# Hybrid decoder step: gate broadcasts and sample attention placed in other stages, second doubled expert one place later

## The chip, the core and the metric

The kernel runs on one core of a Trainium2 chip. The metric is the time on the device of one whole step, in microseconds (us), as the median of several runs. TensorE (PE) does the matrix products into eight PSUM banks, VectorE (DVE) and ScalarE (ACT) read the banks out and do the element work, GpSimd (POOL) does small copies and issues DMAs, SyncE (SP) issues the weight loads. Everything is float32.

## What is computed

One layer for 256 prompt rows and 8 x 4 sample rows, width 2048, cut to the parts that matter here:

```python
h = layernorm(x) * (1 + sc1) + sh1
q, k, v, u = split(h @ w_in)
attn = window_attention(q, k, v, cache)                  # sample rows: 8 requests x 4 positions
z = gelu(s5(u))
ssm = z * sigmoid(z @ ssm_glu_w + ssm_glu_b)
mixed = concat(rms(attn) * attn_norm_g, rms(ssm) * ssm_norm_g)
o = mixed @ w_out
x = layernorm(alpha * x + g1 * o) * ln1_g + ln1_b        # g1: the gate, one row per request
h2 = layernorm(x) * (1 + sc2) + sh2
# mixture: best group of 4, then the best 2 of its 8 experts, 288 rows x 2 = 576 pairs over 32 experts
f = sum_e comb[:, e] * ((silu(h2 @ w_gate[e]) * (h2 @ w_up[e])) @ w_down[e])
x = layernorm(alpha * x + g2 * f) * ln2_g + ln2_b
```

## The kernel before

The program is written out by hand for each engine, with semaphores between them; the order of the code is the order of the queue. The weights pass in 1 MB chunks through a ring: six slots up to the experts, twelve for them. SP loads a chunk when the PE has counted the old one off on the semaphore `used`.

The stages around the change, on the PE:

- **glu stage.** `glu_part(m)`, m = 0 to 7, is one eighth of `z @ ssm_glu_w` (eight matmuls of 128x288, L2346). ACT's `glu_gate(m)` takes the sigmoid (L1271), DVE's `ssm_gated(m)` the product (L1763, L1766) and POOL its square (L1087). After the fourth part stand the turns of q (L2289) and the scores of the sample rows (L2362, L2363), after the eighth the turns of the sample probabilities (L2372).
- **first output projection.** `project(q, half)` is half of the inner width for 512 columns of `mixed @ w_out`: sixteen 128x512 matmul records for the two prompt blocks (L2395) and eight for the samples, four 32-column pieces beside each other (L2398). q = 0 to 3 take the ssm half of `mixed`, and q = 4 to 7 the attention half. q = 0 is run first, both halves.
- **between it and the heads.** Eight matmuls with a column of ones sum the squares of the ssm half (L2435). Then a loop over x = 0 to 7 does three things. It broadcasts the gate g1 over the partitions, for x = 0 to 3 from 32 rows of `MOD` into bank 7 (L2450) and for x = 4 the sample gates (`by_quarters`, L2443), each copied out by ACT into `GX` or `GXs` (L1310) before the next may overwrite the bank. It multiplies the sample probabilities with the cached and the new values of request x (L2457, L2458) into banks 0 to 3. In two of its turns it also adds up the four sample pieces (`sum_parts(0)`, L2406) and turns the row of squares (L2465). After the loop comes one `ada_step` (L348, the weights of the later modulation), then `scores(0)` and `scores(1)` (L2384), which wait until DVE has read the sample attention out (`so_ready`, L1811), and then `project(1, 0)`.
- **heads.** Eight units of prompt attention, each with a half projection, ada steps and turns, up to the second half of the output projection.

DVE reads the sample attention first (L1811), then adds the projection of the prompt blocks (`blocks_out(0)`, L1853 and L1863), then that of the samples (`samples_out(0)`), then the heads.

**Experts.** Each pass of the expert loop is one block of up to 64 rows of one expert: L792 gate and up products, L754 and L761 the gathering of the next block's rows by a selection matrix, L770 their turns, L800 and L809 the down product. Where an expert has more than 64 rows, its second block uses the same weights, and the ring's slots are counted free in the second one only. The order of the experts is by a key: an expert's number, and for the w-th doubled expert WIDE_FROM + WIDE_STEP * w. Experts without rows are left out.

Of the kernel before, what the change touches and what calls it, by code (L numbers as in the profile page):

```python
# [20 lines left out]
ALU = mybir.AluOpType  # L21
ACT = mybir.ActivationFunctionType
AX = mybir.AxisListType

P = 128
# [23 lines left out]
WIDE_FROM, WIDE_STEP = 4.5, 6.0  # L49
# [161 lines left out]
def build(nc, a, o, scratch):  # L211
# [11 lines left out]
    with ExitStack() as ctx:  # L223
# [204 lines left out]
        GX, GXs = later[:, 6144:8192], later[:, 8192:8704]  # L428
# [17 lines left out]
        g_q, b_q = L[:, 8704:9216], L[:, 9216:9728]  # L446
        dot, sq_junk, w_s = L[:, 9728:10752].rearrange("p (i n) -> p i n", i=2), L[:, 10752:11264], L[:, 11264:11776]
# [523 lines left out]
        with nc.Block() as block:  # L971
# [31 lines left out]
            def _(pool):  # L1003
# [96 lines left out]
                for r, x in enumerate(("ln1_g", "ln1_b")):  # L1100
                    pool.dma_start(R4[r:P:NS, :], a[x].rearrange("o (q n) -> (o q) n", q=4)).then_inc(S("r4_in"), 16)
                for x, t in (("ln1_g", g_q), ("ln1_b", b_q)):
# [22 lines left out]
            def _(act):  # L1125
# [148 lines left out]
                for m in range(4):  # L1274
                    glu_gate(m)
# [4 lines left out]
                glu_gate(4)  # L1280
                glu_gate(5)
                act.wait_ge(S("snegmax_ready"), 1)
# [4 lines left out]
                glu_gate(6)  # L1287
                glu_gate(7)
# [14 lines left out]

                act.wait_ge(S("kv_out"), 16 * 20)
                parts_out(0)
                act.wait_ge(S("ssm_ready"), 16)
                act.wait_ge(S("state_out"), 64)
                for i in range(5):
                    act.wait_ge(S("gx_ps"), i + 1)
                    nc.scalar.copy(GX[:, 512 * i:512 * i + 512] if i < 4 else GXs, bank[:, 7, :])\  # L1310
                      .then_inc(S("gx_ready"), 1)
                act.wait_ge(S("rs_ms"), 2)
                nc.scalar.activation(srms[:, :], srms[:, :], ACT.Sqrt).then_inc(S("rs_sqrt"), 1)
# [50 lines left out]
                for i in range(2):  # L1364
                    if i:
                        act.wait_ge(S("kc_ready"), since("kc_ready") + 1)
                    nc.scalar.activation(L[:, 9728:11776], GEf[:, D * i:D * i + D], ACT.Square, accum_out=kc[:, 2 + i:3 + i])\
# [73 lines left out]
            def _(dve):  # L1441
# [365 lines left out]
                dve.wait_ge(S("so_ps"), 1)  # L1807
                for g in range(NKV):
                    r = slice(32 * g, 32 * g + 32)
                    src = bank[r, 0:4, :].rearrange("p j (b n) -> p (j b) n", b=2)[:, :, HD * g:HD * g + HD]  # L1810
                    V.tensor_tensor(OS[r, :, :], src, spread(sden[r, :], HD), ALU.mult).then_inc(S("so_ready"), 1)  # L1811
# [897 lines left out]
```

## Time and profile before

| | us |
|---|---|
| median of 3 runs | 1620.47 |
| lowest and highest | 1614.94, 1621.84 |
| the profiled execution | 1620.20 |
| its span, first to last instruction | 1618.4 |
| PE busy in it | 1499.4 (93%) |
| DVE, ACT, POOL busy | 509.3, 287.2, 142.3 |

Starts are counted in us from the first instruction. The loops and the stages follow each other in time: up to about 341 the front of the layer, 341 to 380 the glu stage, 380 to 396 the first output projection, 396 to 430 the loop of small products, 430 to 676 heads, projection and router, 676 to 1566 the 31 expert blocks, then the last norm.
### The profile page before, as it was taken

The numbers are of one execution on the slowest core, as the hardware profiler recorded it, in microseconds if no ns is written. First come the engines' busy times: TensorE is split into PE (matmuls) and PEld (weight loads), VectorE is DVE, ScalarE is ACT, GpSimd is POOL, SyncE is SP. The second block draws the span as 40 slices with busy tenths as digits, with TensorE's granted clock in tenths as the row PEclk, the third lists the DMA queues.
The fourth block names the chain that finished last, engine by engine and source line by source line (L and its number), as shares of the span: only waits on it lengthen the run. The fifth ranks groups of instructions, "written<-read, shape, count | busy, mean of one in ns | idle before, by whom it ended". The sixth has DMA issues, their size and how long they took to land.

```text
span 1618.4 us, 22163 instructions
## 1 busy us (share of the span) xinstructions
PE 1499.4 (93%) x8151; PEld 641.5 (40%) x8152; DVE 509.3 (31%) x1446; ACT 287.2 (18%) x669; POOL 142.3 (9%) x213
## 2 busy tenths in 40 slices
PE   3899999999999899899999999999999999999974
PEld 2457544455444345333333333333333333333321
DVE  6648354322233356721121212112121211211216
ACT  2221240132222322121121201001010100100111
POOL 6001000320300230000000000000000000000011
PEclk9999999999699899899999999999999999999997
DMA  9995888973287789899999989999799999999955
GB/s 300 387 386 181 305 323 311 316 197 104 61 302 290 290 300 396 359 411 422 421 422 421 378 333 422 422 421 422 297 406 421 421 421 422 422 421 422 421 234 222
DMA packets 119286, 559.66 MB, mean 346 GB/s; under 512 B 15657, under 2 KB 20553, under 8 KB 64921
## 3 DMA queue, kind: packets, MB, share of 16 engines
q1 hardware_dynamic: 100800, 510.20, 79.1%
q0 software_dynamic: 17952, 46.05, 8.4%
q10 hardware_dynamic: 482, 2.70, 0.6%
q8 instruction: 34, 0.56, 0.1%
q14 instruction: 18, 0.15, 0.0%
HBM read 565.78 MB, written 42.37 MB: 376 GB/s over the span
## 4 chain that ended last, share of the span: by engine, by line
PE 79%; DMA 13%; DVE 4%; ACT 2%; issue 1%; POOL 0%; POOLq 0%; SPq 0%; DVEq 0%; ACTq 0%
PE bank L792 24%; PE bank L809 11%; DMA ring<-in_exp_w_up 8%; PE bank L2395 6%; PE bank L754 6%; PE bank L2303 5%; PE bank L2153 4%; PE bank L348 3%; DMA ring<-in_w_in 2%; PE bank L2346 2%; DMA ring<-in_ada_w 2%; PE bank L761 2%; DVE BC L610 1%; PE bank L800 1%; PE bank L2235 1%
## 5 line engine op out<-in xcount | busy, mean ns | idle before, releaser
L792 PE MATMUL bank<-ring,BC 128*64 128x512 f32 x1984 | 473.8, 596 | 5.5 <-DMA ring<-in_exp_w_up 3.2
L792 PEld LDWEIGHTS bank<-ring,BC 128*64 128x64 f32 x1984 | 151.1, 137 | 301.2 <-issue 279.1
L809 PE MATMUL bank<-ring,BC 128*64 128x512 f32 x992 | 219.7, 595 | 16.6 <-ACT BC L715 16.6
L589 DVE COPY MOD<-bank 128x512 f32<-128x512 f32 x32 | 22.1, 692 | 430.3 <-PE bank L761 430.3
L754 PE MATMUL bank<-H,MOD 128*64 128x512 f32 x512 | 132.9, 592 | 0.3 <-DVE H L2013 0.3
L809 PEld LDWEIGHTS bank<-ring,BC 128*64 128x64 f32 x992 | 70.8, 137 | 142.5 <-issue 142.5
L545 POOL DMA_INDIRECT y_dram<-BC,y_row x31 | 29.9, 965 | 947.7 <-DVE y_row L619 862.7
L2395 PE MATMUL bank<-ring,MT 128*128 128x512 f32 x224 | 101.6, 607 | 1.0 <-issue 0.8
L703 ACT COPY MOD<-bank 128x512 f32<-128x512 f32 x32 | 18.7, 585 | 461.9 <-PE bank L761 461.9
L2303 PE MATMUL bank<-ring,MT 128*128 128x512 f32 x192 | 85.4, 598 | 1.0 <-ACT X L1228 1.0
L616 DVE COPY BC<-bank 128x512 f32<-128x512 f32 x31 | 21.4, 692 | 166.1 <-PE bank L809 166.1
L2153 PE MATMUL bank<-MT,ring 128*128 128x288 f32 x256 | 66.0, 421 | 6.3 <-DMA ring<-in_w_in 4.0
L754 PEld LDWEIGHTS bank<-H,MOD 128*64 128x64 f32 x512 | 41.2, 137 | 73.0 <-issue 71.8
L348 PE MATMUL bank<-ring,cT 128*32 128x512 f32 x512 | 65.0, 625 | 0.0
L2395 PEld LDWEIGHTS bank<-ring,MT 128*128 128x128 f32 x224 | 42.2, 193 | 55.4 <-issue 54.8
L2153 PEld LDWEIGHTS bank<-MT,ring 128*128 128x128 f32 x256 | 50.1, 197 | 21.8 <-issue 5.3
L610 DVE TENSOR_TENSOR BC<-BC,bank 64x512 f32<-64x512 f32 x31 | 21.4, 691 | 111.6 <-ACT BC L713 111.6
L719 ACT COPY BC<-bank 128x512 f32<-128x512 f32 x31 | 18.1, 585 | 212.2 <-PE bank L809 212.2
L2303 PEld LDWEIGHTS bank<-ring,MT 128*128 128x128 f32 x192 | 35.6, 190 | 48.1 <-issue 46.9
L2131 PE MATMUL bank<-ring,cT 128*32 128x512 f32 x256 | 36.1, 659 | 19.4 <-DMA ring<-in_ada_w 19.0
L770 PEld LDWEIGHTS bank<-con,MOD 128*128 128x128 f32 x256 | 33.3, 210 | 26.9 <-issue 25.1
L770 PE MATMUL bank<-con,MOD 128*128 128x128 f32 x256 | 39.4, 297 | 0.9 <-DVE MOD L589 0.9
(561 smaller groups left out, 1465.5 us busy)
## 6 DMA issues: line engine op xcount, KB each, us to landing
ring<-in_exp_w_gate SPq DMA_DIRECT2D x128, 1024.0 KB
ring<-in_exp_w_up SPq DMA_DIRECT2D x128, 1024.0 KB
ring<-in_exp_w_down SPq DMA_DIRECT2D x128, 1024.0 KB
ring<-in_ada_w SPq DMA_DIRECT2D x96, 1024.0 KB
ring<-in_w_in SPq DMA_DIRECT2D x20, 1024.0 KB
y_dram<-con POOLq DMA_DIRECT2D x20, 1024.0 KB, 34.2
ring<-in_w_out SPq DMA_DIRECT2D x16, 1024.0 KB
ring<-in_ssm_glu_w SPq DMA_DIRECT2D x4, 1024.0 KB
```

The source lines that it names most:

```text
L348: mm = pe.matmul(bank[32 * g:32 * g + 32, b, :], cT[:, k, :], w[:, 512 * g:512 * g + 512], start=(k == k0), stop=(k == k1))
L610: V.tensor_tensor(AC[hi, :], SG[hi, :], bank[hi, 2, :], ALU.mult).then_inc(S("act_ready"), 1)
L754: pe.matmul(bank[64 * h:64 * h + 64, i, :], sel[:, b, :], H[:, b, 512 * q:512 * q + 512], start=(b == 0), stop=False)
L761: mm = pe.matmul(bank[64 * (q % 2):64 * (q % 2) + 64, q // 2, :], sel[r, 2, :], H[r, 2, 0:512], start=False, stop=True)
L770: mm = pe.transpose(bank[:, i, P * k:P * k + P], XG[:, i, k:512:4], ident)
L792: mm = pe.matmul(bank[64 * i:64 * i + 64, 2, :], xT[:, q // 2, k % 4, 64 * (q % 2):64 * (q % 2) + 64], ring[:, at, 512 * (k % 4):512 * (k ...
L809: mm = pe.matmul(bank[64 * (c % 2):64 * (c % 2) + 64, 4 + c // 2, :], aT[:, j, :], ring[:, at, 512 * c:512 * c + 512], start=(j == 0), sto ...
L2131: mm = pe.matmul(bank[32 * g:32 * g + 32, 4 + v, :], cT[:, 4 * i + g, :], w[:, g, :], start=(i == 0), stop=(i == 3))
L2153: mm = pe.matmul(bank[:, 4 * half + m, 0:T], w[:, k, P * m:P * m + P], MT[:, 4 * j + k, :], start=(j == 0 and k == 0), stop=(j == 3 and k ...
L2303: pe.matmul(bank[:, b, :], MT[:, 4 * i + k, P * b:P * b + P], w[:, k, :], start=(i == 0 and k == 0), stop=(i == 3 and k == 3))
L2346: mm = pe.matmul(bank[:, 4 + m % 2, 0:T], w[:, k, P * (m % 2):P * (m % 2) + P], Z[:, k, :], start=(k == 0), stop=(k == 7))
L2395: pe.matmul(bank[:, x, :], MT[:, k0 + k, P * b:P * b + P], w[:, k, :], start=(half == 0 and k == 0), stop=(half == 1 and k == 3))
```

## The change

It keeps every product, and moves them:

- The four broadcasts of the gate stand behind `glu_part(2)`, `(3)`, `(4)` and `(5)`, that of the samples behind `glu_part(6)`. ACT copies them between its sigmoids. `GX` lies in other columns of the ring (four separate pieces), since the glu stage still uses its old place; `b_q`, `dot` and the junk tile of the squares move likewise, and POOL waits once for `state_out` before it loads over the old state columns.
- The sample attention products stand inside `project(0, 0)` (requests 0 and 1) and `project(0, 1)` (2 to 5), one behind each inner step, and 6 and 7 behind it. The sums of the squares stand between the two halves.
- `scores(0)` and `scores(1)` stand inside `project(1, 0)`, behind its second inner step. The wait for `x_smp` moves from ahead of `project` to ahead of its sample matmuls.
- DVE does `blocks_out(0)` ahead of the reading of the sample attention, and ACT the root of the ssm scale ahead of `parts_out(0)`.
- WIDE_FROM, WIDE_STEP go from 4.5, 6.0 to 2.5, 8.0.

PE, from the first output projection to the ada step behind the loop (its last product being row L348), before. `bank` is PSUM, `MT` the mixed rows turned, `con` the constants, `BC`, `H` and `X` hold probabilities and values:

```order
L2395 MATMUL bank<-ring,MT 128x512 x8
L2398 MATMUL bank<-ring,MT 32x512 x4
L2395 MATMUL bank<-ring,MT 128x512 x8
L2398 MATMUL bank<-ring,MT 32x512 x4
L2435 MATMUL bank<-H,con 1x288 x8
L2450 MATMUL bank<-MOD,con 128x512
L2457 MATMUL bank<-BC,H 128x256
L2458 MATMUL bank<-X 128x256
L2406 MATMUL bank<-BC 32x512
L2450 MATMUL bank<-MOD,con 128x512
L2457 MATMUL bank<-BC,H 128x256
L2458 MATMUL bank<-X 128x256
```

The same place with the change, from the sample matmuls of the first half on:

```order
L2438 MATMUL bank<-ring,MT 32x512 x4
L2498 MATMUL bank<-H,con 1x288 x8
L2431 MATMUL bank<-ring,MT 128x512 x2
L2469 MATMUL bank<-BC,H 128x256
L2470 MATMUL bank<-X 128x256
L2431 MATMUL bank<-ring,MT 128x512 x2
L2469 MATMUL bank<-BC,H 128x256
L2470 MATMUL bank<-X 128x256
L2488 MATMUL bank<-con,H 128x1 x3
L2431 MATMUL bank<-ring,MT 128x512 x2
L2469 MATMUL bank<-BC,H 128x256
L2470 MATMUL bank<-X 128x256
```

The 32-row broadcasts are gone from here, and each pair of small products has two 128x512 matmuls of the projection on either side.

PE, the end of the glu stage with the change, where before the four L2346 parts stood in one piece (a row of 32):

```order
L2358 MATMUL bank<-ring 128x288 x8
L2376 MATMUL bank<-MOD,con 128x512
L2358 MATMUL bank<-ring 128x288 x8
L2376 MATMUL bank<-MOD,con 128x512
L2358 MATMUL bank<-ring 128x288 x8
L2366 MATMUL bank<-MOD,con 32x512 x4
L2358 MATMUL bank<-ring 128x288 x8
```

A broadcast now stands behind each part but the last.

DVE, which frees the banks that the next projection writes, before:

```order
L1811 TENSOR_TENSOR BC<-bank,sden 32x512 [waits so_ps,dve_self]
L1811 TENSOR_TENSOR BC<-bank,sden 32x512 x3
L1853 SCALAR_TENSOR_TENSOR BC<-bank,srms,ring 128x512 [waits used,gx_ready,xa_in]
L1863 SCALAR_TENSOR_TENSOR ring<-ring,BC 128x512 [waits out_free]
L1853 SCALAR_TENSOR_TENSOR BC<-bank,srms,ring 128x512 [waits dve_self]
```

and with the change:

```order
L1864 SCALAR_TENSOR_TENSOR BC<-bank,srms,ring 128x512 [waits gx_ready,used,xa_in,dve_self]
L1874 SCALAR_TENSOR_TENSOR ring<-ring,BC 128x512 [waits out_free]
L1864 SCALAR_TENSOR_TENSOR BC<-bank,srms,ring 128x512 [waits dve_self]
L1874 SCALAR_TENSOR_TENSOR ring<-ring,BC 128x512 [waits out_free]
L1822 TENSOR_TENSOR BC<-bank,sden 32x512 [waits so_ps,dve_self]
L1822 TENSOR_TENSOR BC<-bank,sden 32x512 x3
```

The two groups have changed places.

The diff, cut to its core:

```diff
-WIDE_FROM, WIDE_STEP = 4.5, 6.0
+WIDE_FROM, WIDE_STEP = 2.5, 8.0
...
-        GX, GXs = later[:, 6144:8192], later[:, 8192:8704]
+        GX = [later[:, at:at + 512] for at in (4608, 5120, 5632, 9216)]
+        GXs = later[:, 9728:10240]
...
+                def gx_out(i):
+
+                    act.wait_ge(S("gx_ps"), i + 1)
+                    nc.scalar.copy(GX[i] if i < 4 else GXs, bank[:, 7, :]).then_inc(S("gx_ready"), 1)
+
+                glu_gate(0)
+                glu_gate(1)
+                glu_gate(2)
+                gx_out(0)
+                glu_gate(3)
+                gx_out(1)
...
                 glu_gate(4)
+                gx_out(2)
                 glu_gate(5)
+                gx_out(3)
...
                 glu_gate(6)
+                gx_out(4)
                 glu_gate(7)
...
+                act.wait_ge(S("rs_ms"), 2)
+                nc.scalar.activation(srms[:, :], srms[:, :], ACT.Sqrt).then_inc(S("rs_sqrt"), 1)
                 act.wait_ge(S("kv_out"), 16 * 20)
                 parts_out(0)
...
                 blocks_out(0)
+                samples_attended()
                 samples_out(0)
...
                 for m in range(4):
                     glu_part(m)
+                    if m >= 2:
+                        gx_in(m - 2)
...
                 for m in range(4, 8):
                     glu_part(m)
+                    if m < 7:
+                        gx_in(m - 2)
...
-                def project(q, half):
+                def project(q, half, between=None):
...
+                        if between:
+                            between(k)
+                    if half == 0 and 0 < q < 4:
+                        pe.wait_ge(S("x_smp"), q)
...
+                project(0, 0, first_samples)
+                for m in range(8):
+                    pe.wait_ge(S("sq_ready"), m + 1)
+                    mm = pe.matmul(bank[0:1, 3, 0:T], ones[:, 0:1], gate[:, m, :], start=(m == 0), stop=(m == 7))
+                mm.then_inc(S("rs_ps"), 1)
+                pe.wait_ge(S("ssm_ready"), 16)
+                project(0, 1, middle_samples)
+                pe.wait_ge(S("rs_ms"), 2)
+                samples_attend(6)
+                samples_attend(7)
+                pe.wait_ge(S("sum4_ready"), 1)
+                sum_parts(0)
                 pe.wait_ge(S("gx_ready"), 5)
                 for v, k in ADA_FIRST:
                     ada_step(pe, v, k, 7)
...
-                        project(q, i % 2)
+                        project(q, i % 2, None if i else first_scores)
```

## Rows read from the trace of the kernel before

**Rows 1.** The page: clock granted to the PE in 40 slices of 40.5 us.

```profile
PEclk9999999999699899899999999999999999999997
```

**Rows 2.** Timeline of PE, 396 to 454: start us, us, engine, line, product, records [idle before <-releaser].

```profile
396.37 4.04 PE L2435 MATMUL bank<-H,con 128*1 128x288 f32 x16
400.34 1.12 PE L2450 MATMUL bank<-MOD,con 32*128 32x512 f32 x2
401.39 0.70 PE L2457 MATMUL bank<-BC,H 128*128 128x256 f32 x2
...
402.65 1.05 PE L2406 MATMUL bank<-BC 128*32 128x512 f32 x2
...
426.68 3.09 PE L2384 MATMUL bank<-H,GE 64*128 64x128 f32 x16 [1.14 <-DVE BC L1811]
430.52 8.95 PE L2395 MATMUL bank<-ring,MT 128*128 128x512 f32 x16 [0.75 <-issue]
...
440.29 1.04 PE L348 MATMUL bank<-ring,cT 128*32 128x512 f32 x8
...
444.73 1.16 PE L2384 MATMUL bank<-H,GE 64*128 64x128 f32 x8
445.82 7.13 PE L2395 MATMUL bank<-ring,MT 128*128 128x512 f32 x16
...
453.88 0.44 PE L2415 MATMUL bank<-con,X 128*128 128x128 f32 x2
```

**Rows 3.** Stretches: length, busy us (records) of PE, PEld, DVE, ACT, POOL, PEclk, DMA share, GB/s.

```profile
400.00:405.00 5.00, 5.00 (x14) 1.61 (x12) 0.61 (x2) 0.80 (x2) 0.00 (x0) 1.00 0.21 81
405.00:410.00 5.00, 5.00 (x18) 2.12 (x16) 0.16 (x1) 0.95 (x2) 0.00 (x0) 0.69 0.00 0
415.00:420.00 5.00, 5.00 (x10) 2.00 (x8) 0.18 (x1) 2.90 (x4) 0.00 (x0) 0.50 0.00 0
...
430.00:435.00 5.00, 4.48 (x6) 1.98 (x7) 4.65 (x13) 1.74 (x9) 5.00 (x9) 0.58 0.17 20
```

**Rows 4.** Timeline of PE: turns of the next rows (L770), one row per expert block.

```profile
696.78 1.23 PE L770 MATMUL bank<-con,MOD 128*128 128x128 f32 x8
...
893.83 1.23 PE L770 MATMUL bank<-con,MOD 128*128 128x128 f32 x8
...
923.59 1.23 PE L770 MATMUL bank<-con,MOD 128*128 128x128 f32 x8
...
1374.09 1.23 PE L770 MATMUL bank<-con,MOD 128*128 128x128 f32 x8
...
1403.85 1.23 PE L770 MATMUL bank<-con,MOD 128*128 128x128 f32 x8
...
1556.07 1.23 PE L770 MATMUL bank<-con,MOD 128*128 128x128 f32 x8
```

**Rows 5.** Stretches of one block's length in the experts, columns as in rows 3.

```profile
921.98:950.13 28.15, 27.28 (x133) 9.92 (x131) 5.01 (x16) 2.62 (x5) 0.96 (x1) 1.00 0.63 244
...
1147.18:1175.33 28.15, 27.27 (x135) 10.19 (x133) 5.01 (x16) 2.62 (x5) 0.96 (x1) 1.00 0.60 239
```

**Rows 6.** Timeline of PE: a broadcast by quarters at the full clock.

```profile
570.80 1.06 PE L2443 MATMUL bank<-MOD,con 32*32 32x512 f32 x8
```

**Rows 7.** Timeline of PE in the middle of the glu stage.

```profile
357.20 1.04 PE L2289 MATMUL bank<-con,X 128*128 128x128 f32 x8
...
360.65 0.45 PE L2362 MATMUL bank<-ring,X 64*32 64x128 f32 x8 [1.75 <-POOL X L1082]
...
363.10 15.79 PE L2346 MATMUL bank<-ring 128*128 128x288 f32 x64
```

**Rows 8.** Timeline of ACT: one copy of a gate broadcast.

```profile
401.58 0.58 ACT L1310 COPY ring<-bank 128x512 f32<-128x512 f32 x1 [4.32 <-PE bank L2450]
```

**Rows 9.** Timeline of DVE behind the loop of small products.

```profile
423.78 2.84 DVE L1811 TENSOR_TENSOR BC<-bank,sden 32x512 f32<-32x512 f32 x4 [6.93 <-PE bank L2458]
426.66 0.75 DVE L1853 SCALAR_TENSOR_TENSOR BC<-bank,srms,ring 128x512 f32<-128x512 f32 x1
427.44 0.69 DVE L1863 SCALAR_TENSOR_TENSOR ring<-ring,BC 128x512 f32<-128x512 f32 x1
```

More of the change, by code:

```diff
@@ L1806, in _, with samples_attended @@
                 go(V.reciprocal(srms[:, :], srms[:, :]))
[L1807 to L1811, printed above, removed]
+                def samples_attended():
+                    dve.wait_ge(S("so_ps"), 1)
+                    for g in range(NKV):
+                        r = slice(32 * g, 32 * g + 32)
+                        src = bank[r, 0:4, :].rearrange("p j (b n) -> p (j b) n", b=2)[:, :, HD * g:HD * g + HD]
+                        V.tensor_tensor(OS[r, :, :], src, spread(sden[r, :], HD), ALU.mult).then_inc(S("so_ready"), 1)
                 def head(i):
@@ L2348, in glu_part, with by_quarters, gx_in @@
                     mm.then_inc(used if m % 2 else S("glu_ps"), 1)
+                def by_quarters(b, v, at):
+                    for g in range(4):
+                        r = slice(32 * g, 32 * g + 32)
+                        mm = pe.matmul(bank[r, b, :], con[r, C_SEL + at:C_SEL + at + NS], MOD[r, v, :], start=True, stop=True)
+                    return mm
+                def gx_in(x):
+                    if x:
+                        pe.wait_ge(S("gx_ready"), x)
+                    else:
+                        pe.wait_ge(S("y_free"), 8)
+                    if x < 4:
+                        mm = pe.matmul(bank[:, 7, :], con[32 * x:32 * x + 32, C_SEL:C_SEL + P],
+                                       MOD[32 * x:32 * x + 32, 0, :], start=True, stop=True)
+                    else:
+                        mm = by_quarters(7, 0, P)
+                    mm.then_inc(S("gx_ps"), 1)
                 pe.wait_ge(S("z_ready"), 2)
@@ L2424, in samples_in, with samples_attend @@
                     mm.then_inc(S("mt_ps"), 1)
[L2426 to L2455 removed]
+                def samples_attend(x):
                     out = bank[:, x // 2, 256 * (x % 2):256 * (x % 2) + 256]
@@ L2458, in _, with first_samples, middle_samples @@
                     mm = pe.matmul(out, PTn[:, x, :], qkv[0:NS, 2, DA + DKV:DA + 2 * DKV], start=False, stop=True)
-                    if x == 0:
-                        pe.wait_ge(S("sum4_ready"), 1)
-                        sum_parts(0)
-                    if x == 1:
+                    if x == 7:
+                        mm.then_inc(S("so_ps"), 1)
+                def first_samples(k):
+                    if k == 1:
+                        pe.wait_ge(S("spt_ready"), 4)
+                        samples_attend(0)
+                    elif k == 2:
+                        samples_attend(1)
+                def middle_samples(k):
+                    samples_attend(2 + k)
+                    if k == 1:
                         pe.wait_ge(S("rs_ms"), 1)
@@ L2467, in _ @@
                         rs.then_inc(S("rs_ps"), 1)
-                mm.then_inc(S("so_ps"), 1)
+                pe.wait_ge(S("glu_sig"), 8)
+                pe.wait_ge(S("mod_ready"), 2)
+                pe.wait_ge(S("ssm_ready"), 8)
+                project(0, 0, first_samples)
[10 more added lines that the diff above has]
+                sum_parts(0)
                 pe.wait_ge(S("gx_ready"), 5)
@@ L2471, in _, with first_scores @@
                     ada_step(pe, v, k, 7)
+                def first_scores(k):
+                    if k == 1:
+                        scores(0)
+                        scores(1)
                 unit_end = {4: KD - 1, 5: ADA_LAST[0][1] - 1}
-                scores(0)
                 for i, (n, g) in enumerate(UNITS):
-                    if i < 7:
+                    if 0 < i < 7:
                         scores(i + 1)
```

49 lines of the change are left out of this document (6 added, 43 removed).

## The prediction

> **What bounds the kernel now.** I read the page's clock row first: the PE is busy 93% of the span, so time is lost where it works slowly. One slice early in the program stands at 6 tenths, the eleventh, 405 to 445 us [rows 1]. The stretches of 5 us say where: the PE is busy without a gap from 400 to 420, yet its granted clock is 1.00 up to 405, 0.69 in the next 5 us, 0.50 at 415 (1.2 GHz, the lower of its two levels) and still 0.58 at 430 to 435 [rows 3]. The timeline shows what it did before: from 396.37 on it ran the sums with a column of ones, then 32-row broadcasts and 256-column products, and nothing dense until `project(1, 0)` at 430.52 [rows 2]. That projection took 8.95 us there and 7.13 at 445.82. So from 396.37 to 440.29, 43.92 us, the bound is the PE at a low clock, and at the end of it two small waits, 1.14 us for DVE's reading of the sample attention and 0.75 us. DMA moves nothing there (share 0.00), since the ring is full.
>
> The experts are the second place. The turns of one block follow those of the next after 28.15 us while the PE is the bound: from 923.59 to 1374.09 there are 16 steps, 450.50 us. From 1403.85 to 1556.07 there are five, 30.44 us each: there the weights bound, 2.29 us more per block. Two single steps, 893.83 to 923.59 and 1374.09 to 1403.85, are 29.76 us, 1.61 over the fast pace [rows 4]. The DMA share falls to 0.63 and 0.60 in two stretches 225 us apart [rows 5]: the doubled experts, whose first block frees no slot. DMA idles 10.4 us in the first and 11.3 us in the second. Nothing between the two stages waits on a date: each load goes by `used`, so what the front gains, the end gains.
>
> **The change part by part.** I sum the profiled execution, 1620.20 us against a median of 1620.47.
>
> *The stretch 396.37 to 440.29.* The same work at the full clock, from rows at 1.00: sums with ones 3.97 (to the next start, 400.34); eight pairs of sample products, each 402.65 - 401.39 = 1.26, together 10.1; the three tiny turns of the square row about 0.3; `sum_parts(0)` 1.05; ada step 1.04; two `scores`, each 445.82 - 444.73 = 1.09, together 2.2; `project(1, 0)` as its neighbour, 453.88 - 445.82 = 8.06 [rows 2]. Sum 26.7. Against 43.9 this takes off 17.2.
>
> *The broadcasts in the glu stage.* Four of 1.05 (401.39 - 400.34) [rows 2] and one by quarters of 1.06 [rows 6]: 5.3 us are added, since the PE has no idle time there that could hide them, except 1.75 us ahead of the sample scores. That wait is no cover: it ends with POOL's copies, which follow ACT's copies of the turned q, and ACT now does one gate copy of 0.58 [rows 8] ahead of those. I add 0.3 (bounds 0 and 0.6). The other ACT copies fall between sigmoids that are 3.9 us apart (15.79 for four parts, [rows 7]), and bank 7 is free long before the next broadcast.
>
> *New waits.* The sample products wait for ACT's copies of the turned probabilities, a full inner step of the projection earlier than they are asked for. The turn of the squares waits for DVE's copies, with two inner steps and two pairs, some 6 us, as cover. `scores(0)` waits for `so_ready`: with P the end of `project(0, 1)`, DVE does four operations of 0.75 and 0.69 (3.0 us), then the four reads, 2.84 us [rows 9], done at P + 5.9. The PE has two pairs (2.5), the sum and the ada step (2.1) and half a projection (3.6) ahead of it, so it asks at P + 8.2: 2.3 us of cover. `out_free` is there at P + 2.3, asked at P + 4.6. Queued behind DVE's wait for `so_ps` are `samples_out(0)` and the first head; `project(1, 0)` asks for `x_smp` only at its samples, some 6 us later. POOL's sample DMAs start later against the projection by some 5 us, and the sample heads are wanted five units on. I cost all of it at nothing. If the cover failed everywhere, 3 us would go back, my upper bound.
>
> *The order of the experts.* The key of the w-th doubled expert goes from 10.5 and 16.5 to 10.5 and 18.5. By the reference's routing of these inputs experts 1 and 6 are doubled (97 and 101 pairs) and 18 has no rows, so the first stays ninth in line and the second passes expert 17 only: one place. After a full ring eight blocks run at 28.15, the ninth waits 1.61, each further one 2.29: so it is from the start (696.78 to 893.83, seven steps of 28.15, then 29.76) and behind the second doubled expert [rows 4]. Before: 1.61 once, then none ahead of the second, then 1.61 and five of 2.29, 14.7 us. After: 1.61 three times (the second doubled expert's first block is now a ninth one) and four of 2.29, 14.0 us. It gains 0.7; the difference of the two idle times, 0.9, says the same. Bounds: 0 and 2.3, one late block.
>
> Sum: -17.2 + 5.3 + 0.3 - 0.7 = -12.3 us. 1620.5 - 12.3 = **1608.2 us**, some 1608.
>
> *A rule against it.* What decides is why the clock fell, and the row shows it falling with no idle time on the PE [rows 3]. The Trainium skill, page "TensorE: Matmul & The Clock Gate", section "Why this matters for your kernels", says that drops amid a kernel are avoided by leaving no idle gaps between bursts of matmuls; by that rule the order of busy work is nothing to the clock. The trace does not agree: no gap, and 0.50. If something else than the kind of work drives it, the change moves work from slow to slow, and that is the second rival.
>
> **The rivals.**
>
> *The clock falls behind the first projection after all.* Two pairs, the sum and the ada step are still light, 4.6 us, and half of `project(1, 0)` comes before more. Price: 4.6 us more for them and 1.8 for the projection (8.95 against 7.13). Gain 5.9: 1614.6. For it: 4 us of ones and then ten of light work brought the fall. Against: the light stretch from 440.29 to 445.82 (ada steps, turns, scores) is 5.5 us and the projection behind it ran in 7.13 [rows 2].
>
> *The fall does not come from the small products.* Then the slow stretch stays with this part of the program, and only the two waits (1.9), the experts (0.7), less 0.3, are gained: 1618.2. For it: the broadcasts and products are counted as full busy time. Against: the lone stretch at 0.50 is the one without dense work.
>
> *The glu stage loses its clock.* Its light part, 357.20 to 363.10, 5.9 us at full clock [rows 7], has a 32-row broadcast ahead of it now. A fall near its end costs its last 2 us and the first 2.6 of the next part, some 4 us: 1612.
>
> *Slower.* The pairs between the steps of `project(0, 1)` bring the clock down inside it. Then 8.06 of projection, six pairs (7.6), the square turns, the sum and the ada step (2.4) run at half speed, 18 us more, and 1.8 in `project(1, 0)`. Net +7.5: 1628. It decides from the point where more than 12.3 us of this work run at 1.2 GHz, so the fall must come before the third inner step. Against: each 1.26 us pair has 1.8 us of dense work on either side, and one dense projection (8.95 us, from 430.52) was enough to bring the clock back before.
>
> **How the numbers follow.** Forecast 0.71, the fall behind the projection 0.10, no clock gain 0.06, a fall in the glu stage 0.07, slower 0.05, more than I sum (other low slices, such as the fourteenth, shift too) 0.01. The forecast's own range is 1605 to 1611: the bounds above and the spread of medians. To hold 8 in 10 the range takes in the glu case and reaches to the first rival: 1604 to 1615. A measurement of this kernel tells some 0.5%, 8.1 us, from no change: faster is under 1612.4, the forecast and most of the glu case, 0.76; within 0.5% the two clock rivals and the rest, 0.19; slower 0.05.
>
> **What would show it.** PEclk's eleventh slice at 9; stretches at 1.00 from 385 to 430; the first projection from some 386, `project(1, 0)` over 11.6 us earlier than 440.29; broadcasts at 1.05 us in the glu stage; no wait at the first `scores`; the wait of 1.75 at about 2.0; the second dip of the DMA share one block later against the first, and four slow blocks at the end for five. Wrong would make it a clock under 1.00 in the glu stage or the first projection, or a wait of the PE for `so_ready`.

## The result and the profile after

The changed kernel takes 1608.71 us (median of 8 executions, 1607.57 to 1612.44); the kernel before 1621.55 (8, 1614.94 to 1623.4). The ratio is 0.9929, 95% interval 0.9919 to 0.9939. The forecast was 1608 with a range of 1604 to 1615.

The profiled execution took 1608.62, its span 1606.8 against 1618.4. The page's clock row, changed kernel:

```profile
PEclk9999999999999898899999999999999999999987
```

The eleventh slice, the 6 of [rows 1], is a 9. The stretches of 5 us (columns as in [rows 3]):

```profile
400.00:405.00 5.00, 5.00 (x15) 2.18 (x14) 0.61 (x2) 0.00 (x0) 0.00 (x0) 1.00 0.27 115
405.00:410.00 5.00, 5.00 (x19) 2.83 (x19) 0.34 (x2) 0.20 (x1) 0.00 (x0) 1.00 0.00 0
415.00:420.00 5.00, 5.00 (x20) 1.91 (x20) 4.77 (x8) 1.40 (x2) 0.00 (x0) 1.00 0.70 229
...
430.00:435.00 5.00, 5.00 (x36) 2.88 (x36) 1.22 (x3) 0.59 (x1) 0.16 (x1) 1.00 0.92 367
```

PE is busy throughout in both kernels up to 420; what changed is the granted clock, 1.00 where [rows 3] has 0.69 and 0.50. The timeline of PE of the changed kernel, beside [rows 2] and [rows 7]:

```profile
341.57 11.88 PE L2358 MATMUL bank<-ring 128*128 128x288 f32 x48 [0.40 <-issue]
353.38 1.12 PE L2376 MATMUL bank<-MOD,con 32*128 32x512 f32 x2
354.43 4.15 PE L2358 MATMUL bank<-ring 128*128 128x288 f32 x16
...
359.56 1.09 PE L2301 MATMUL bank<-con,X 128*128 128x128 f32 x8
...
363.07 0.45 PE L2396 MATMUL bank<-ring,X 64*32 64x128 f32 x8 [1.75 <-POOL X L1083]
...
365.51 4.15 PE L2358 MATMUL bank<-ring 128*128 128x288 f32 x16
369.59 1.12 PE L2376 MATMUL bank<-MOD,con 32*128 32x512 f32 x2
...
386.57 3.60 PE L2431 MATMUL bank<-ring,MT 128*128 128x512 f32 x8
...
402.72 0.59 PE L2469 MATMUL bank<-BC,H 128*128 128x256 f32 x2
403.24 0.69 PE L2470 MATMUL bank<-X 32*128 32x256 f32 x2
403.87 1.98 PE L2431 MATMUL bank<-ring,MT 128*128 128x512 f32 x4
...
418.68 3.70 PE L2431 MATMUL bank<-ring,MT 128*128 128x512 f32 x8
422.31 1.71 PE L2420 MATMUL bank<-H,GE 64*128 64x128 f32 x16
423.95 3.70 PE L2431 MATMUL bank<-ring,MT 128*128 128x512 f32 x8
...
428.46 1.04 PE L348 MATMUL bank<-ring,cT 128*32 128x512 f32 x8
```

The ada step behind `project(1, 0)` starts at 428.46, 11.83 us ahead of the 440.29 of [rows 2]. The scores at 422.31 have no wait in front of them.

**Most of the gain is clock.** Each execution comes with its span and its mean granted clock. Span x (1 - mean clock), called "missing" below, adds up the clock that was not granted; span x mean clock is the rest. (The clock is given to 0.001, which is 1.6 us, so only medians of several executions are worth reading.) Over all executions taken of both kernels in this study:

| | executions | span, us | mean clock | missing, us | span x mean clock, us |
|---|---|---|---|---|---|
| before | 66 | 1618.8 (1610.3 to 1624.3) | 0.971 (0.966 to 0.978) | 47.0 | 1571.5 |
| changed | 12 | 1606.9 (1605.7 to 1610.6) | 0.9785 (0.975 to 0.981) | 34.6 | 1572.3 |

The two kernels differ in the missing clock and hardly in the rest. The measure is rough, since it covers the whole program and also counts a low clock while PE waits, which costs nothing. In the two traces it falls by only 6.7 us (mean clock 0.972 and 0.976) for 11.6 us of span: from 396 to 441 the clock goes from 0.70 to 1.00, but behind the last full turns of the expert loop it is 0.78 before (from 1556) and 0.73 with the change (from 1544). The time that the low clock cost is read from the stretch itself: 43.92 us from 396.37 to 440.29, less 1.9 of waits and less 32.0 of work at the full clock (the 26.7 of the prediction and 5.3 of broadcasts), leaves 10.0 us. So of the 11.6 some 10 are clock, and 1.9 are the waits that went; the smaller terms nearly cancel. The spread of the kernel before, 14 us, goes with the clock as well: its quickest execution has the highest mean clock.

### The profile page after: what moved, and what is told of

It reads as the page before. It is cut to its first block, busy times and chain, and to the rows that moved or that the text cites. A ratio compares the mean times of both kernels' runs of the same rounds, so it can differ in the third digit from the quotient of the medians.

```text
span 1606.8 us, 22161 instructions
## 1 busy us (share of the span) xinstructions
PE 1493.3 (93%) x8151; PEld 645.8 (40%) x8152; DVE 509.9 (32%) x1446; ACT 288.0 (18%) x669; POOL 142.6 (9%) x213
## 4 chain that ended last, share of the span: by engine, by line
PE 79%; DMA 13%; DVE 3%; ACT 2%; issue 1%; POOL 0%; SPq 0%; POOLq 0%; DVEq 0%; ACTq 0%
PE bank L793 24%; PE bank L810 11%; DMA ring<-in_exp_w_up 8%; PE bank L2431 6%; PE bank L755 6%; PE bank L2315 5%; PE bank L2165 4%; PE bank L348 3%; DMA ring<-in_ada_w 3%; PE bank L2358 2%; PE bank L762 2%; DMA ring<-in_w_in 2%; DVE BC L611 1%; PE bank L801 1%; PE bank L2143 1%
## 5 line engine op out<-in xcount | busy, mean ns | idle before, releaser
L348 PE MATMUL bank<-ring,cT 128*32 128x512 f32 x512 | 65.2, 620 | 0.0
L2431 PEld LDWEIGHTS bank<-ring,MT 128*128 128x128 f32 x224 | 40.9, 190 | 51.8 <-issue 51.0
L2315 PEld LDWEIGHTS bank<-ring,MT 128*128 128x128 f32 x192 | 35.6, 190 | 48.1 <-issue 46.9
```

The costliest lines, as they stand in the source:

```text
L348: mm = pe.matmul(bank[32 * g:32 * g + 32, b, :], cT[:, k, :], w[:, 512 * g:512 * g + 512], start=(k == k0), stop=(k == k1))
L2315: pe.matmul(bank[:, b, :], MT[:, 4 * i + k, P * b:P * b + P], w[:, k, :], start=(i == 0 and k == 0), stop=(i == 3 and k == 3))
L2431: pe.matmul(bank[:, x, :], MT[:, k0 + k, P * b:P * b + P], w[:, k, :], start=(half == 0 and k == 0), stop=(half == 1 and k == 3))
```

## The experiments

The theory: the light row behind the first output projection (sums with ones, broadcasts, sample pairs, partial sums, ada step) brings the clock down, and the change cuts it up. Rivals: one piece of that row is the cause (the 32-row broadcasts, A; the one-column sums ahead of the rest, C), or the kind of work does not matter. Two lengths in the traces are compared below: the glu stage, up to the start of `project(0, 0)` (38.86 us before, 45.00 with the change), and the stretch from there to the ada step behind `project(1, 0)` (59.82 and 41.89).

**The order of the experts.** `e1_front` is the changed kernel with the old key, `e2_wide` the kernel before with the new one, `e5_after_again` the changed kernel once more, on another chip.

```diff
-WIDE_FROM, WIDE_STEP = 2.5, 8.0
+WIDE_FROM, WIDE_STEP = 4.5, 6.0
```

> The changed kernel with WIDE_FROM, WIDE_STEP back at 4.5, 6.0: the front's moves alone. My theory: all but the experts' part of the gain, so some 1609 us, and in the trace the loop of expert blocks takes as long as before, 859.3 us from the first to the last turn (L771 rows), against 858.2 with the change. Rival, the order of the experts brings the gain: 1620.

> The kernel before with WIDE_FROM, WIDE_STEP 2.5, 8.0 alone. My theory: 0.7 us less, which the times can't tell (1621), and the expert blocks in the trace take 858 to 858.7 us from first to last turn instead of 859.3. Rival: 1610 with the front's gain in it.

> The changed kernel again, beside the kernels that are to be compared with it: 1608 to 1610 us, granted clock 1.00 from 385 to 435 us.

Measured: `e1_front` 1609.8 (10 executions, 1608.05 to 1611.1), ratio 0.9955 (0.9936 to 0.9974); `e2_wide` 1621.61, ratio 1.0015 (0.9997 to 1.0033); `e5_after_again` 1608.62 (4, 1608.42 to 1610.47), ratio 0.9926 (0.99 to 0.9952). From the first full turns of the expert loop to the last, the traces have 859.29 us before [rows 4], 858.94 in `e2_wide`, 858.52 in `e1_front`, and 858.16 and 858.78 in two executions of the changed kernel. Two traces with one key differ by 0.8, as much as the keys do, so what the new key is worth is not shown; expected were 859.3 in `e1_front` and 858 to 858.7 in `e2_wide`. The times came as expected in all three runs, and the gain is in the front. `e1_front` and `e5_after_again` have a stretch of 41.89 us at a clock of 1.00, as in the changed kernel's first trace. The trace of `e2_wide` has the front of before in the same order, and its clock falls later:

```profile
410.00:415.00 5.00, 5.00 (x22) 1.96 (x21) 0.17 (x1) 3.27 (x5) 0.00 (x0) 1.00 0.01 3
415.00:420.00 5.00, 4.87 (x15) 1.38 (x14) 1.83 (x3) 0.52 (x1) 0.00 (x0) 0.59 0.00 0
```

Its stretch is 53.73 us for the 59.82 of [rows 2]. One order of work thus loses 10 us to the clock in one execution and some 4 in another, and one trace can't rank two orders that differ by less.

**Only the broadcasts moved.** `e3_gx_only` is the changed kernel with the broadcasts in the glu stage, and the rest of the front as before: the sums with ones and all eight pairs in a row behind the whole projection, the scores ahead of `project(1, 0)`, DVE and ACT in the old order.

```diff
-                project(0, 0, first_samples)
+                project(0, 0)
+                pe.wait_ge(S("ssm_ready"), 16)
+                project(0, 1)
...
+                for x in range(8):
+                    samples_attend(x)
...
+                scores(0)
```

> Gate broadcasts in the glu stage; the rest of the front as before (sums with ones and all eight pairs of sample products behind the whole first projection, scores ahead of project(1, 0), old order on DVE and ACT), experts as changed. Theory A, the clock fell because of the 32-row broadcasts: it stays at 1.00, the stretch costs its 26.7 us plus 1.9 of waits for DVE, 5.6 in the glu stage: 10 us less than before, 1611. Theory B, it fell because nothing dense ran for about ten us, whatever the small products were: it falls again 9 to 10 us behind the end of the projection, some 10 us of work run at 1.2 GHz, and 1.8 more in project(1, 0): the gain is gone, 1619 to 1622.

Measured: 1617.65 (1615.76 to 1620.66), ratio 0.9996 (0.9978 to 1.0014). Its stretches, with no broadcast anywhere near:

```profile
405.00:410.00 5.00, 5.00 (x17) 1.80 (x16) 0.61 (x2) 0.09 (x1) 0.00 (x0) 1.00 0.50 193
410.00:415.00 5.00, 5.00 (x19) 2.63 (x18) 0.34 (x2) 1.49 (x2) 0.00 (x0) 0.80 0.01 3
415.00:420.00 5.00, 5.00 (x10) 2.40 (x10) 0.00 (x0) 0.00 (x0) 0.00 (x0) 0.50 0.00 0
```

PE has no gap and the clock goes to 0.50 all the same, so the 32-row broadcasts are not needed for the fall, and theory A in its strict form is gone. The median lies between theory A's 1611 and theory B's 1619 to 1622, 2.5 us under the 1620.18 of before on the same chip (missing 43.6 us against 46.9). The broadcasts cost their 5 us in the glu stage as they did in the row, and the ratio's interval takes in 1: a gain from them alone is not shown.

**Only the pairs, sums and scores moved.** `e4_samples_only` is the changed kernel with the five broadcasts behind the projection, between and behind pairs 6 and 7.

```diff
+                gx_in(0)
                 samples_attend(6)
+                gx_in(1)
                 samples_attend(7)
+                gx_in(2)
...
                 sum_parts(0)
+                gx_in(3)
+                gx_in(4)
```

> Sample products, sums with ones and scores inside the projections as changed; the gate broadcasts not in the glu stage but behind the first projection, between the last two pairs and the sum. The broadcasts cost the same 5.3 us there, and DVE's blocks_out(0) waits for the last copy, 2.3 us more on the PE. Theory A (32-row broadcasts): the clock falls in them, 3 to 6 us more: 1614 to 1617. Theory B (a long run without dense work): the light run is 10 us and the wait 2.3, just long enough: also 1612 to 1617. If the clock stays at 1.00: 1611.

Measured: 1611.8 (1610.27 to 1614.6), ratio 0.9948 (0.9929 to 0.9966). The light row is 8.7 us of work and 1.9 of waits, two of them for ACT's copies. The clock is 0.82 in 415 to 420 and 0.50 in 420 to 425, and the first half of `project(1, 0)` takes 5.81 us for 3.70. The median lies by the lower ends of all three expectations, so it does not tell the theories apart:

```profile
416.51 1.06 PE L2363 MATMUL bank<-MOD,con 32*32 32x512 f32 x8 [0.68 <-ACT ring L1279]
418.28 1.93 PE L348 MATMUL bank<-ring,cT 128*32 128x512 f32 x8 [0.70 <-ACT ring L1279]
420.74 5.81 PE L2424 MATMUL bank<-ring,MT 128*128 128x512 f32 x8 [0.53 <-DVE BC L1861]
```

So most of the gain (8 of 12 us) comes from the pairs, sums and scores. The broadcasts' move adds about 3: their 5 us are paid in the glu stage in place of the row, and the waits (1.9) and the last fall (2.1) go.

**All eight pairs in a row.** `e6_row` is the changed kernel with the eight pairs behind the projection; the sums stay between its halves and the broadcasts in the glu stage.

```diff
-                    samples_attend(2 + k)
...
-                samples_attend(6)
-                samples_attend(7)
+                for x in range(8):
+                    samples_attend(x)
```

> The changed kernel with all eight pairs of sample products in a row behind project(0, 1), instead of between its steps; the sums with ones stay between the halves, the broadcasts in the glu stage. Light work behind the projection: samples 1.0, eight pairs 10.1, sum and ada step 2.1, 13 us, none of it a 32-row broadcast. By the theory that the clock falls after some ten us without dense work: it falls near the last pairs, the rest of them and the sum and the ada step (about 4 us) and part of project(1, 0) run slow: 5 to 6 us more than the changed kernel, 1614. If what counts is not the run of light work but its place among other things: 1609.

Measured: 1612.78 (7 executions, 1610.68 to 1615.45), ratio 0.9954 (0.9934 to 0.9973). The size came as expected for a fall in the row, but the trace shows another cause: its row of pairs runs from 410.63 to 422.49 with the clock at 1.00, and the fall stands in the glu stage, at the scores of the sample rows:

```profile
365.00:370.00 5.00, 5.00 (x100) 4.48 (x92) 1.84 (x7) 0.00 (x0) 1.04 (x2) 0.55 0.02 3
415.00:420.00 5.00, 5.00 (x17) 2.36 (x16) 0.00 (x0) 0.00 (x0) 0.00 (x0) 1.00 0.05 17
```

The glu stage takes 47.78 us for 45.00, and the stretch 42.47 for 41.89. The traced execution is the median one (1612.78), so the 4 us over the changed kernel do not show that a row of pairs costs clock; whether it does in the other six executions is open. Theory C, tested below, came from the 1.00 in this row.

**The broadcasts twice.** `e7_gx_twice` issues each of the five broadcasts twice in the glu stage.

```diff
+                    for again in range(2):
```

> Each gate broadcast is issued twice in the glu stage, the first one without effect on the output. If the glu stage has no cover for them, as I summed, 5.3 us more than the changed kernel: 1614. If it hides them (rival): 1609. If the 2.1 us of light work more bring the clock down amid the stage: 1618.

Measured: 1613.74 (1611.05 to 1617.42), ratio 0.9957 (0.994 to 0.9973), 5.1 us over the changed kernel, as expected: nothing in the glu stage covers a broadcast. Four broadcasts went from 1.05 to 1.91 us start to start, the one by quarters from 0.99 to 1.85, so doubling them costs 4.3; the trace's glu stage is 5.85 longer, the rest being a dip of the clock at the sample scores, of which below.

**DVE in the old order.** `e8_dve_old` is the changed kernel with the sample attention read ahead of `blocks_out(0)`.

```diff
-                blocks_out(0)
                 samples_attended()
+                blocks_out(0)
                 samples_out(0)
```

> The changed kernel with DVE in the old order, the reading of the sample attention ahead of blocks_out(0). With P the end of project(0, 1), out_free comes at P + 7.7 instead of P + 2.3 and the PE asks at P + 4.4: a wait of 3.3 us, so 1612. If the PE's idle time adds to the light work before it and the clock falls: 1614 to 1616.

Measured: 1614.09 (1610.51 to 1617.9), ratio 0.9953 (0.9936 to 0.997), 5.5 us over the changed kernel and in the range expected for a wait with a fall of the clock. Timeline of PE:

```profile
416.04 1.44 PE L348 MATMUL bank<-ring,cT 128*32 128x512 f32 x5
420.97 5.40 PE L2431 MATMUL bank<-ring,MT 128*128 128x512 f32 x8 [3.50 <-DVE BC L1864]
```

DVE's reading of the pairs (2.84 us) now stands ahead of the reading of the banks that `project(1, 0)` overwrites. PE waits 3.50 us, and the half projection behind takes 5.40 us for 3.70, at a clock of 0.66 in 420 to 425. So a true gap behind light work lowers the clock too. On this the trace agrees with the row of the Trainium skill that the prediction argued with (page "TensorE: Matmul & The Clock Gate", section "Why this matters for your kernels"); a gap is one way down and not the only one. The swap on DVE, costed at nothing in the prediction, carries 5 us of the gain once the scores are out of the way: without it the cover that the prediction counted on is gone.

**Where the sums stand.** `e9_ones_mid` is the kernel before with only the sums (and the wait for `spt_ready`) moved between the projection's halves. `e10_row_late` is `e6_row` with the sums behind the projection, directly ahead of the pairs.

```diff
                 project(0, 0)
+                pe.wait_ge(S("spt_ready"), 4)
+                for m in range(8):
+                    pe.wait_ge(S("sq_ready"), m + 1)
+                    mm = pe.matmul(bank[0:1, 3, 0:T], ones[:, 0:1], gate[:, m, :], start=(m == 0), stop=(m == 7))
+                mm.then_inc(S("rs_ps"), 1)
                 pe.wait_ge(S("ssm_ready"), 16)
                 project(0, 1)
```

> The kernel before with one edit: the sixteen one-column sums of squares (4.0 us of TensorE) stand between the two halves of the first output projection and not behind it; the five broadcasts, the eight attention pairs, the partial sums and the first ADA products stay behind it in a row, some 19 us at the full clock. Theory C (the clock falls behind the projection because the one-column sums stand directly ahead of more light work; pairs behind dense work alone did not bring it down in the run with all eight pairs in a row): the granted clock stays at 1.00 up to the scores and the time falls by most of the 17 us that the low clock costs, to 1604 to 1608. Theory D (any light row longer than some 12 us brings the clock down): it falls in the last third of the row, 1611 to 1615. Theory A (the 32-row broadcasts bring it down): it falls some 6 us into the row, 1614 to 1618.

> The changed kernel with all eight attention pairs in a row behind the first output projection, as in the run before that had them so, and now the sixteen one-column sums directly ahead of them as well: 4 us of sums, 10 us of pairs, 2 us of partial sums and ADA products, no broadcasts. Only the place of the sums differs from the run with the row (1612.8, clock 1.00 throughout the row). Theory C: the clock falls during the pairs, some 10 us into the light row (409 to 413 us), about 6 us of light work at half speed and a piece of project(1,0): 1617 to 1621. Theory that the place of the sums does not matter: 1612 to 1614 and clock 1.00.

Measured: `e9_ones_mid` 1619.63 (10 executions, 1614.97 to 1622.88), ratio 1.0001 (0.9985 to 1.0017); mean clock 0.971, missing 46.9 us. No theory's range holds it (1604 to 1608, 1611 to 1615, 1614 to 1618). Its clock falls as before:

```profile
405.00:410.00 5.00, 5.00 (x20) 2.16 (x18) 0.16 (x1) 1.17 (x2) 0.00 (x0) 0.87 0.13 48
410.00:415.00 5.00, 5.00 (x14) 1.69 (x14) 0.00 (x0) 0.94 (x2) 0.00 (x0) 0.50 0.02 3
```

`e10_row_late`: 1612.9 (4 executions, 1610.14 to 1619.42), ratio 0.9948 (0.9928 to 0.9969). The traced one is the slowest of the four (span 1617.6, mean clock 0.969) and its pairs slow down from 413.8 on (1.22 us for 0.70); its stretch is 49.99 us. The others have 0.976 to 0.978. Its trace alone would speak for theory C. The medians speak against it: moving the sums by themselves brings nothing in the kernel before, and putting them back costs nothing that four executions can show. As the only cause, the place of the sums is out.

**Broadcasts from all rows.** `e11_gx128` is the kernel before with the four gate broadcasts taken from 128 rows in place of 32. They then give the sum of four quarters of the gate, so the hidden state is another, and the router sends the rows elsewhere: two more expert blocks are computed (2112 records of gate and up products for 1984), and its total of 1671.88 can't be compared.

```diff
-                        pe.matmul(bank[:, 7, :], con[32 * x:32 * x + 32, C_SEL:C_SEL + P],
-                                  MOD[32 * x:32 * x + 32, 0, :], start=True, stop=True).then_inc(S("gx_ps"), 1)
+                        pe.matmul(bank[:, 7, :], con[:, C_SEL:C_SEL + P],
+                                  MOD[:, 0, :], start=True, stop=True).then_inc(S("gx_ps"), 1)
```

> The kernel before with the four gate broadcasts taken from all 128 rows in place of 32 (each then gives the sum of the four quarters of the gate, so this part of the output differs); same order, same column count, same number of instructions. Theory A (few rows lit bring the clock down): clock 1.00 at least until the last broadcast, 4 to 17 us less than before, 1604 to 1617. Theory C (the sums ahead and the length of the row): the clock falls as before near 406, no change, 1620 to 1623.

Its light row has the order and the instructions of before, and no gap up to 418:

```profile
405.00:410.00 5.00, 5.00 (x21) 2.89 (x19) 0.16 (x1) 1.25 (x3) 0.00 (x0) 1.00 0.00 0
410.00:415.00 5.00, 5.00 (x22) 1.92 (x20) 0.17 (x1) 3.46 (x5) 0.00 (x0) 1.00 0.02 3
...
420.00:425.00 5.00, 2.87 (x18) 2.19 (x19) 4.79 (x7) 0.00 (x0) 4.80 (x9) 0.70 0.51 182
```

The clock stays up to the first true wait (2.01 us, ahead of the scores) behind the row. All four executions have a mean clock of 0.975 to 0.979 (missing 39.2 us) where the 13 of the kernel before on this chip have 0.966 to 0.976 (48.5). Up to the scores only the number of rows that four matmuls use was changed, so the mean clocks say that this counts. That rests on four executions, and the trace adds little: its stretch is 53.21 us, and `e2_wide` with the 32-row broadcasts has 53.73 and a clock of 1.00 up to 415. So that the kind of light work counts is likely and not shown beyond doubt.

**What the runs say together.** The light row behind the projection, in us of work at the full clock (for before from the trace of `e11_gx128`, 396.92 to 417.95, and the scores, 1.71), the stretch with its clock in the one trace of each kernel, and the missing clock of the whole program over all executions. Where the broadcasts stand in the row, the stretch holds 5.2 us more of work, and the glu stage as much less:

| kernel | light row | stretch, us | clock in it | executions | missing, us |
|---|---|---|---|---|---|
| before | 22.7 | 59.82 | 0.77 | 66 | 47.0 |
| `e2_wide` | 22.7 | 53.73 | 0.87 | 10 | 51.8 |
| `e11_gx128` | 22.7 | 53.21 | 0.94 | 4 | 39.2 |
| `e9_ones_mid` | 18.7 | 56.92 | 0.82 | 10 | 46.9 |
| `e3_gx_only` | 18.5 | 52.21 | 0.80 | 10 | 43.6 |
| `e10_row_late` | 16.6 | 49.99 | 0.83 | 4 | 38.7 |
| `e6_row` | 11.9 | 42.47 | 1.00 | 7 | 40.3 |
| `e4_samples_only` | 8.7 | 51.30 | 0.93 | 10 | 37.0 |
| changed | 4.4 | 41.89 | 1.00 | 12 | 34.6 |

The clock fell with PE busy in all five traces with 16.6 us or more of light work in a row and 32-row or no broadcasts in it. With PE's order of the changed kernel in the stretch and no new gap it was 1.00 in all five traces (both of the changed kernel, `e1_front`, `e7_gx_twice`, `e12_better`), each 41.89 us long. By this the cause is that the light work stands in a row; neither the broadcasts (`e3_gx_only`) nor the place of the sums (`e9_ones_mid`) is it alone. How long a row may be is not shown: the one trace of `e6_row` holds the clock, and `e4_samples_only` loses it around its waits. The last column moves by other stages too, and by some us between medians of ten (`e2_wide` misses 51.8 with the row of before), so neighbours in it can't be told apart.

**The next light stretch filled.** `e12_better` is the changed kernel, and the main products of `project(4, 0)` stand as four steps between the light work of unit 7.

```diff
+                def last_step(k):
...
+                    w = arrived(pe, first[("out", 0, 0)]).rearrange("p (m n) -> p m n", m=4)
+                    for b in range(2):
+                        pe.matmul(bank[:, b, :], MT[:, k, P * b:P * b + P], w[:, k, :], start=(k == 0), stop=False)
...
+                    if i == 7:
+                        last_step(0)
                     if i:
                         heads_in(i - 1)
+                    if i == 7:
+                        last_step(1)
```

> The changed kernel, and the main products of the first half of project(4,0), which stood behind the last attention unit, are spread as four steps of 0.93 us over the light work of units 6 and 7, where TensorE waits for 0.59, 0.76, 1.16 and 0.59 us at 528 to 538 us and the granted clock is 0.71, 0.50 and 0.77 in the slices from 530 to 543. If the first chunk of the second output weight has landed by 529 us: up to 3.1 us of waits filled and about 3 us of low clock gone, 1602 to 1606. If it lands later, TensorE waits for it ahead of the softmax's own work and the gain turns: 1609 to 1615.

Measured: 1606.06 (4 executions, 1604.16 to 1606.72), at the upper end of the 1602 to 1606 expected, ratio to before 0.9909 (0.9891 to 0.9927). Every span (1602.3 to 1604.9) is under every span of the changed kernel (1605.7 and more), on another chip. The stretches of `e12_better`, and behind them of the changed kernel:

```profile
530.00:545.00 15.00, 15.00 (x81) 7.34 (x80) 1.99 (x9) 4.60 (x12) 7.48 (x14) 1.00 0.82 287
...
640.00:662.00 22.00, 20.50 (x102) 7.45 (x94) 14.52 (x59) 1.45 (x3) 0.00 (x0) 0.73 0.94 371
```

```profile
530.00:545.00 15.00, 12.65 (x57) 7.15 (x58) 1.99 (x9) 4.48 (x12) 7.50 (x14) 0.66 0.82 297
...
640.00:662.00 22.00, 20.55 (x106) 7.32 (x106) 16.82 (x71) 0.59 (x1) 0.00 (x0) 0.82 1.01 423
```

The weights were there, the waits are filled and the clock stays. The second projection's halves end at 551.05 for 559.16, 8.1 us ahead. But only 5.7 are left at the router (630.39 for 636.10) and 2.2 at the first expert (659.86 for 662.08): the router's own light work ran at a lower clock in this execution. Over the four executions span x mean clock is 5 us less than the changed kernel's (1567.1), and the missing clock 2 us more (36.9).

## Why the prediction held, step by step

- **The stretch** was to give 17.2 us. From the start of `project(0, 0)` to the ada step behind `project(1, 0)` it took 440.29 - 380.47 = 59.82 before and 428.46 - 386.57 = 41.89 after: 17.93. The 0.7 more come from sizes: six pairs between dense steps take 1.15 each (403.87 - 402.72), not the 1.26 of [rows 2], and the two scores 1.64 together (423.95 - 422.31), not 2.2; the broken projection gives about half of that back. The 17.2 rest on one trace of the kernel before. With the trace of `e2_wide`, whose front has the same order and a stretch of 53.73, the same sum would have forecast 6 us less of a gain; that the trace at hand lay at the median (1620.20 for 1620.47) was luck that the prediction did not price.
- **The broadcasts in the glu stage** were to cost 5.3, and 0.3 for the chain of the turned q. The stage took 380.47 - 341.61 = 38.86 before and 386.57 - 341.57 = 45.00 after: 6.14. The broadcasts are 5.2 of it. The chain cost 0.06 (turns to sample scores 3.51 for 3.45, the wait 1.75 in both), so that term was too high. What I had not costed is the break itself: a part of the glu takes 4.08 us where a broadcast follows (365.51 to 369.59) and 3.91 in a row (four parts from 363.10 to 378.72, [rows 7]), five times 0.17. The stage cost 0.5 more than summed and the stretch gave 0.7 more, so part of the closeness of 1608.2 to 1608.71 is chance.
- **New waits at nothing:** right. DVE was to be done with the sample attention 2.3 us ahead of the scores; it was 1.9:

```profile
414.57 0.75 DVE L1864 SCALAR_TENSOR_TENSOR BC<-bank,srms,ring 128x512 f32<-128x512 f32 x1 [6.46 <-PE bank L2438]
...
417.60 2.84 DVE L1822 TENSOR_TENSOR BC<-bank,sden 32x512 f32<-32x512 f32 x4
```

  (done at 420.44, asked for at 422.31). The price named for a lost cover, 3 us, was too small: by `e8_dve_old` it is 5.5, since the wait takes the clock with it.
- **The experts** were to gain 0.7 by four slow steps for five. The turns of the changed kernel, beside [rows 4]:

```profile
882.68 1.23 PE L771 MATMUL bank<-con,MOD 128*128 128x128 f32 x8
...
912.08 1.23 PE L771 MATMUL bank<-con,MOD 128*128 128x128 f32 x8
...
1137.27 1.23 PE L771 MATMUL bank<-con,MOD 128*128 128x128 f32 x8
...
1166.25 1.23 PE L771 MATMUL bank<-con,MOD 128*128 128x128 f32 x8
...
1363.29 1.23 PE L771 MATMUL bank<-con,MOD 128*128 128x128 f32 x8
...
1391.49 1.23 PE L771 MATMUL bank<-con,MOD 128*128 128x128 f32 x8
1421.95 1.23 PE L771 MATMUL bank<-con,MOD 128*128 128x128 f32 x8
...
1543.76 1.23 PE L771 MATMUL bank<-con,MOD 128*128 128x128 f32 x8
```

  The form failed and the size came near. Against 28.15 the steps are 1.25 over at 882.68, 0.83 over at 1137.27, nothing at 1363.29 (28.20), and then five at 30.45, not four. 13.7 us of waits in all, forecast 14.0, before 14.8; but 14.3 in the second trace of the changed kernel, and 14.0 in `e1_front` with the old key, so the traces don't confirm the 0.7. The slips at the ninth blocks are smaller than the 1.61 that I took for each, and the ring's lead behind the second doubled expert ran out one block earlier.
- **Where the rest went.** The gain is 11.83 at 428.46, 11.18 at the first full turns (685.60 for 696.78) and 11.6 over the span. The front's gain reaches the end but for 0.65 us lost between 428 and 686: the ring was full at the change and the loads go by `used`.
- **The cause** held in the form of the forecast, light work without dense work. Of the rivals, the second (the fall does not come from the small products) falls by the result itself: the same pairs, sums and scores in the same stretch, PE busy in both, and the clock at 1.00 in all five traces with the new order. The first (a fall behind the projection after all) is seen in no trace of the changed kernel; in `e4_samples_only`, with the broadcasts there, and in `e8_dve_old`, with a gap, it comes. The third, a fall in the glu stage, exists in some executions: the stretch 365 to 370 is at 0.56 in `e1_front`, which has PE's order of the changed kernel, and the stretch 360 to 365 at 0.66 in `e2_wide` and `e9_ones_mid`, which have the old order there; the traces of before and of the changed kernel have 1.00 there. So it comes without the broadcasts too, but it costs more with them: the glu stage takes 47.56 us in `e1_front`, 47.78 in `e6_row` and 47.68 in `e10_row_late` for 45.00, and 40.46 in `e2_wide` for 38.86. The prediction priced it at 4 us and at 0.07; it stood in three of the eight traces that have the broadcasts there once.

What stays open is which of the small products weighs how much, how long a row of them may be, and why one execution of the same program keeps the clock in a row in which another loses it.

## What to carry to other kernels

Where a page shows a slice with PE busy and PEclk low, look at what the matmuls are, not at the waits: light products (few rows, few columns) do best one by one between dense ones, and a row of them at the end of a dense stage costs twice, by itself and in the dense work behind it. Before you judge by one trace, look at whether it is a typical execution: one order of the front lost 10 us to the clock in one trace and 4 in another, and the trace of `e10_row_late` is of its slowest execution. Span x (1 - mean clock) over all executions shows a large difference, but it mixes all stages: of the extra 4 us of `e6_row`, 2.8 stood in a stage that the edit did not touch. And when PE's order is tightened, the reader of its banks has to be put in the order in which PE asks next: a swap of two groups on DVE was worth 5 us here.

## What the runs showed of the hardware

- The granted clock goes to 0.50 with PE busy in every us (`e3_gx_only`, 415 to 420), and it keeps 1.00 up to the first wait where four of the matmuls use 128 rows for 32 at about the same length (`e11_gx128`, 400 to 418); with the 32 rows it fell from 405 on in one trace and from 415 on in another (`e2_wide`).
- The same program on the same input has a mean clock of 0.966 to 0.978 over 66 executions, and the span follows it from 1624.3 down to 1610.3.
- A row of 128x288 matmuls that is broken by another product loses some 0.17 us at the break; a pair of 256-column products costs 1.15 us between dense steps and 1.26 in a row of its like.
- Clock won at one light stretch was partly lost at the next (`e12_better`: 8.1 us won at 551, 2.2 left at 660).
